# Two-layer PEER encoder kernel: scores of four heads at the 11th query block, and the search in two parts

## The reference, cut to what matters

```
q = (ht @ w_q).reshape(T, PEER_HEADS, 2, PEER_HALF_DIM)      # 8 heads, two halves of 128
scores = einsum('thic,hikc->thik', q, sub_keys)              # 128 keys for each half
sv, si = top_k(scores, 16)
cand = sv[:, :, 0, :, None] + sv[:, :, 1, None, :]
best, ci = top_k(cand.reshape(T, 8, 256), 16)
expert = i1 * 128 + i2;  gate = softmax(best)                # 128 experts for each token
hid = gelu(x . w_down[expert]);  out = sum(gate * hid * w_up[expert])
```

## Time and profile before

| | us |
|---|---|
| median of 3 runs | 1507.93 (1506.27 to 1508.06) |
| the profiled execution, whole | 1518.31 |
| its span | 1516.5 |
| PE busy | 1485.6 |
| DVE busy | 886.0 |
| POOL busy | 715.4 |
| ACT busy | 476.5 |
| granted TensorE clock, mean | 0.997 |

### The profile page before, as it was taken

The page is one execution under the profiler, slowest core; times in us unless marked ns, Lnnn a source line. Parts: engine busy times, 40 slices in busy tenths (PEclk is TensorE's granted clock), DMA queues, the critical chain, the costliest instruction groups (busy, mean ns, idle before and its releaser), DMA issues.

```text
span 1516.5 us, 29050 instructions
## 1 busy us (share of the span) xinstructions
PE 1485.6 (98%) x10668; PEld 1445.1 (95%) x10668; DVE 886.0 (58%) x2901; ACT 476.5 (31%) x1200; POOL 715.4 (47%) x632
## 2 busy tenths in 40 slices
PE   7999999999999999999999999999999999999996
PEld 6889999999999999999988999999999999999995
DVE  1740989947885444444623339997488834444463
ACT  5654231238881000000156532221688500000001
POOL 6577033348995233333457731333699823323350
PEclk9999999999999999999999999999999999999999
DMA  6456988999999999999945579899999999999993
GB/s 239 147 193 230 333 316 334 408 408 352 388 380 404 416 416 416 417 417 414 361 139 202 205 247 344 320 409 409 363 374 383 387 418 415 416 417 417 416 399 131
DMA packets 126417, 523.12 MB, mean 345 GB/s; under 512 B 14817, under 2 KB 15073, under 8 KB 109537
## 3 DMA queue, kind: packets, MB, share of 16 engines
q1 hardware_dynamic: 56896, 240.27, 41.8%
q0 software_dynamic: 55296, 201.35, 34.0%
q10 hardware_dynamic: 14112, 80.04, 12.9%
HBM read 519.48 MB, written 1.05 MB: 343 GB/s over the span
## 4 chain that ended last, share of the span: by engine, by line
PE 91%; DMA 3%; issue 2%; ACT 2%; POOL 2%; DVE 0%; DVEq 0%; ACTq 0%; POOLq 0%
PE ps L993 90%; DMA spare<-in_wu 1%; POOL w_lo L599 1%; DMA arena<-in_rows,ret 1%; PE ps L1001 1%; ACT w_hi L686 0%; DMA xs<-in_x 0%; ACT arena L674 0%; DMA raw<-in_wm 0%; POOL arena L616 0%; ACT arena L745 0%; ACT hT_hi L701 0%; ACT L664 0%; DVE arena L1510 0%; ACT ret L903 0%
## 5 line engine op out<-in xcount | busy, mean ns | idle before, releaser
L993 PE MATMUL ps<-arena,w_raw 128*128 128x160 f32 (+1 forms) x2688 | 381.1, 300 | 4.0 <-issue 2.3
L993 PE MATMUL ps<-arena,raw 128*128 128x160 f32 (+1 forms) x2688 | 377.5, 299 | 0.2
L993 PEld LDWEIGHTS ps<-arena,w_raw 128*128 128x128 f32 x2688 | 369.7, 191 | 6.3 <-issue 6.2
L993 PEld LDWEIGHTS ps<-arena,raw 128*128 128x128 f32 x2688 | 368.1, 190 | 0.7 <-issue 0.7
L616 POOL DMA_INDIRECT arena<-in_up_rows,ret x192 | 187.4, 976 | 358.5 <-DVE oh_buf L1684 267.0
L616 POOL DMA_INDIRECT arena<-in_rows,ret x192 | 199.9, 1041 | 295.1 <-ACT ret L880 104.5
L1684 DVE SCALAR_TENSOR_TENSOR oh_buf<-arena,ret,oh_buf 128x1024 f32<-128x1024 f32 x126 | 161.9, 1285 | 230.2 <-DMA arena<-in_up_rows,ret 224.6
L599 POOL TENSOR_TENSOR w_lo<-raw,w_hi 128x1024 fp32r<-128x1024 f32 x80 | 194.0, 2434 | 93.3 <-PE ps L993 66.3
L993 PE MATMUL ps<-arena 128*128 128x160 f32 (+5 forms) x1336 | 184.5, 302 | 2.1 <-DMA spare<-in_wu 2.1
L993 PEld LDWEIGHTS ps<-arena 128*128 128x128 f32 (+2 forms) x1336 | 177.9, 189 | 5.8 <-issue 4.4
L1567 DVE SCALAR_TENSOR_TENSOR arena<-arena,ps 128x1024 f32<-128x1024 f32 x128 | 153.6, 1212 | 0.0
(11 more groups left out here) (146 smaller groups left out, 1788.4 us busy)
## 6 DMA issues: line engine op xcount, KB each, us to landing
raw<-in_wd SPq DMA_DIRECT2D x92, 512.0 KB
w_raw<-in_wd SPq DMA_DIRECT2D x92, 512.0 KB
raw<-in_wm SPq DMA_DIRECT2D x80, 512.0 KB
low_rows<-in_wu SPq DMA_DIRECT2D x18, 1024.0 KB
arena<-in_wu SPq DMA_DIRECT2D x18, 1024.0 KB
arena<-in_wd SPq DMA_DIRECT2D x32, 512.0 KB, 5.0
raw<-in_wu SPq DMA_DIRECT2D x14, 1024.0 KB
raw<-in_wu ACTq DMA_DIRECT2D x14, 1024.0 KB
```

The costliest lines, as they stand in the source:

```text
L993: return nc.tensor.matmul(out, lhsT, rhs, start=start, stop=stop, skip_group_check=shared)
```

## The change

**Scores of four heads early.** Before the 11th query block (`b == EARLY_SCORES_BEFORE` = 10) PE computes tile 0's scores of heads 0 to 3, into banks 0 and 1; ACT copies them after `high` of block 12. The other scores follow after the query blocks; tile 0's heads 4 to 7 use banks 0 and 1 again and wait for ACT's copies.

**Search in parts.** DVE searches heads 0 to 3 of tile 0, then heads 4 to 7, then tile 1. The first part uses PSUM banks 2 and 3, so the row products of tile 0 (`h_rows`, banks 2 and 3, before down block 8) now wait for `pair_found` of that part. Dots are put from the last steps of the second part on: 44 in 20 places. A piece of picks is now two neighbouring heads (heads i and i + 4 before).

**Places.** The pieces are taken before blocks 4, 7, 20 and 25 (18, 21, 24 and 26 before), ids at 71 (77), gates from block 74 (80), the dots of the gate stage are 52 over 50 blocks (56 over 44). The ring starts at slot 2, since slots 0 and 1 lie on the scores of tile 0, and POOL's tenth gather waits until both parts of the scores have been searched. SP may load the up pair that lies on ring slots 8 and 9 after 88 dots (90 before).

```diff
-RING, IN_FLIGHT = 10, 5
+RING, IN_FLIGHT, RING_FIRST = 10, 5, 2
...
-IDS_AT = 77
-TAKE_AT = 26
-PIECES, PIECE_AT = 4, (18, 21, 24, 26)
-MORE_AT, MORE_TAKE_AT, MORE_GATES_AT = 28, 33, 40
+IDS_AT = 71
+TAKE_AT = 28
+PIECES, PIECE_AT = 4, (4, 7, 20, 25)
+EARLY_SCORES_BEFORE, EARLY_HEADS = 10, RH // 2
+SCORE_BANKS = (0, 1, 0, 1, 4, 5, 6, 7)
+MORE_AT, MORE_TAKE_AT, MORE_GATES_AT = 26, 34, 40
-G_FROM = 80
+G_FROM = 74
-ONES_FROM, ROWS_AT, ONES = 12, 8, 432
-SPARSE_FIRST, MORE_LAST = 18, 10
-EARLY, EARLY_PLACES = SPARSE_FIRST + MORE - MORE_LAST, 14
+ONES_FROM, ROWS_AT, ONES = 30, 8, 432
+SPARSE_FIRST, MORE_LAST = 26, 14
+EARLY, EARLY_PLACES = SPARSE_FIRST + MORE - MORE_LAST, 20
-    return EARLY + max(0, min(ROWS - EARLY, (b - G_FROM - 1) * (ROWS - EARLY) // 44))
+    return EARLY + max(0, min(ROWS - EARLY, (b - G_FROM - 1) * (ROWS - EARLY) // 50))
...
-        slot = q % RING if q < ROWS else (q - ROWS) % UP_RING
+        slot = (q + RING_FIRST) % RING if q < ROWS else (q - ROWS) % UP_RING
...
-        first_sv = ps[:, 5, 0:P].rearrange("p (h k) -> p h k", h=RH)
-        first_id = ps[:, 5, P:2 * P].rearrange("p (h k) -> p h k", h=RH)
+        def search_psum(bank, heads):
+            firsts = ps[:, bank, 0:2 * heads * TOPK].rearrange("p (i h k) -> p i h k", i=2, h=heads)
+            pay = ps[:, bank + 1, 0:heads * CAND].rearrange("p (h c) -> p h c", h=heads)
+            return firsts[:, 0], firsts[:, 1], pay
...
-                sp.wait_ge(row_used, l * GATHERS + ROWS - ROWS % RING)
+                sp.wait_ge(row_used, l * GATHERS + ROWS - (ROWS + RING_FIRST) % RING)
...
+                    if q == RING - 1:
+                        pool.wait_ge(first_searched, l + 1)
...
+                def take_scores(i):
+                    act.wait_ge(sc_psum, 8 * l + i + 1)
+                    nc.scalar.activation(scores[i // 4][:, i % 4 * 512:(i % 4 + 1) * 512], ps[:, SCORE_BANKS[i], :],
+                                         ACT.Copy, scale=rinv[:, 2, i // 4:i // 4 + 1]).then_inc(sc_sb, 1)
+
                 take_queries(0)
-                high_parts(l * LAYER + Q_FROM + 12, l * LAYER + MIX_BLOCKS)
+                act.wait_ge(rinv_done, query_norm)
+                for b in range(Q_FROM + 12, MIX_BLOCKS):
+                    high(b)
+                    if b == Q_FROM + EARLY_SCORES_BEFORE + 2:
+                        take_scores(0)
+                        take_scores(1)
                 take_queries(1)
-                act.wait_ge(rinv_done, query_norm)
-                for i in range(8):
-                    act.wait_ge(sc_psum, 8 * l + i + 1)
-                    nc.scalar.activation(scores[i // 4][:, i % 4 * 512:(i % 4 + 1) * 512], ps[:, i, :], ACT.Copy,
-                                         scale=rinv[:, 2, i // 4:i // 4 + 1]).then_inc(sc_sb, 1)
+                for i in range(2, 8):
+                    take_scores(i)
 
                 def take_hidden(b):
...
-                        first = half * PICKS + i * size
+                        first = (2 * i + half) * size
...
                     transpose_half(xs, 4, hT_psum, k, HALF_BANKS)
+                def score(t, halves):
+                    for n in halves:
+                        o = n % 4 * P
+                        last = mm(ps[:, SCORE_BANKS[4 * t + n // 4], o:o + P], qT[:, n, t * P:(t + 1) * P],
+                                  subk[:, n, :])
+                        if n % 4 == 3:
+                            last.then_inc(sc_psum, 1)
...
+                    if b == EARLY_SCORES_BEFORE:
+                        pe.wait_ge(subk_loaded, 16 * (l + 1))
+                        pe.wait_ge(qT_sb, 8 * l + 4)
+                        score(0, range(2 * EARLY_HEADS))
                     if b == NORMED_BEFORE:
                         pe.wait_ge(hn_done, QUARTERS * (l + 1))
...
-                pe.wait_ge(subk_loaded, 16 * (l + 1))
-                for t in range(TILES):
-                    for n in range(HALVES):
-                        if n % 4 == 0:
-
-                            pe.wait_ge(qT_sb, 8 * l + (8 if t else max(4, n // 2 + 2)))
-                        o = n % 4 * P
-                        last = mm(ps[:, 4 * t + n // 4, o:o + P], qT[:, n, t * P:(t + 1) * P], subk[:, n, :])
-                        if n % 4 == 3:
-                            last.then_inc(sc_psum, 1)
+                for n in range(2 * EARLY_HEADS, HALVES, 4):
+                    pe.wait_ge(qT_sb, 8 * l + n // 2 + 2)
+                    pe.wait_ge(sc_sb, 8 * l + n // 4 - 1)
+                    score(0, range(n, n + 4))
+                pe.wait_ge(qT_sb, 8 * (l + 1))
+                score(1, range(HALVES))
...
                     if b < SLOTS:
-                        pe.wait_ge(sc_sb, 8 * l + DOWN_BANKS[slot] + 1)
+                        pe.wait_ge(sc_sb, 8 * l + 3 + slot)
...
-                pe.wait_ge(sc_sb, 8 * l + 4)
+                pe.wait_ge(pair_found, PIECES * l + PIECES // 2)
...
-
-                for t in range(TILES):
-                    dve.wait_ge(sc_sb, 8 * l + 4 * (t + 1))
+                def early_dot():
+                    if not early[0]:
+                        dve.wait_ge(h_rows_psum, l + 1)
+                        dve.wait_ge(more_rows_sb, 16 * PARTS * (l + 1))
+                    dots(early_after(early[0] - 1), early_after(early[0]))
+                    early[0] += 1
+
+                def search(t, h0, h1, ready, bank, dots_from):
+
+                    heads, halves = slice(h0, h1), range(2 * h0, 2 * h1)
+                    first_sv, first_id, pay = search_psum(bank, h1 - h0)
+                    dve.wait_ge(sc_sb, 8 * l + ready)
                     top16([(scores[t][:, n * KEYS:(n + 1) * KEYS], sv[:, t, n, :], si[:, t, n, :])
-                           for n in range(HALVES)], t)
+                           for n in halves], t, dots_from < 1)
                     settle()
-                    step(nc.vector.tensor_copy(sif[:, t].rearrange("p h i k -> p (h i) k"), si[:, t]))
-                    svt = sv[:, t].rearrange("p (h i) k -> p h i k", i=2)
-                    if t == 0:
+                    found_ids = nc.vector.tensor_copy(
+                        sif[:, t, heads].rearrange("p h i k -> p (h i) k"), si[:, t, 2 * h0:2 * h1])
+                    if t == 0 and h0:
+                        found_ids.then_inc(first_searched, 1)
+                        dve.wait_ge(first_searched, l + 1)
                         dve.wait_ge(sc_sb, 8 * (l + 1))
                         dve.wait_ge(hng_done, l + 1)
                         step(nc.vector.tensor_copy(numbers, iota[:, :]))
...
-                        h = j // 4 + j // 2 % 2 * (RH // 2)
+                        h = j // 2
...
-                            early_dot(t)
+                        if j % 2 and dots_from < 3:
+                            early_dot()
...
+                gates_of(1)
 
                 dve.wait_ge(idg_psum, l + 1)
                 step(nc.vector.tensor_copy(gT, ps[:, 5, 0:SEQ]))

```

More of the change, by code:

```diff
@@ L886, in take_gates @@
                     for half in range(2):
-                        here, picks = slice(half * SPARSE, (half + 1) * SPARSE), slice(half * PICKS, (half + 1) * PICKS)
-                        nc.scalar.activation(row_gate[here], bb[0:SPARSE, picks], ACT.Copy).then_inc(gates_taken, 1)
+                        here = slice(half * SPARSE, (half + 1) * SPARSE)
+                        picks = bb[0:SPARSE, 0:P].rearrange("p (i h k) -> p h i k", h=2, k=TOPK)[:, half]
+                        nc.scalar.activation(row_gate[here].rearrange("p (i k) -> p i k", k=TOPK), picks,
+                                             ACT.Copy).then_inc(gates_taken, 1)
                 def take_more_picks():
@@ L1523, in _, with top16 @@
                 norm_tokens()
-                def top16(rows, t):
+                def top16(rows, t, with_dots):
                     for r in range(0, len(rows), 8):
@@ L1598, in _ @@
                         na = a1 - a0
-                        for dst, first, second in ((cand, first_sv, svt), (pay, first_id, sif[:, t])):
+                        for dst, first, second in ((cand[:, heads], first_sv, svt), (pay, first_id, ids)):
                             d = dst[:, :, o:o + na * nb].rearrange("p h (a b) -> p h a b", b=nb)
-                            f = first[:, :, a0:a1].unsqueeze(3).to_broadcast([P, RH, na, nb])
-                            s = second[:, :, 1, 0:nb].unsqueeze(2).to_broadcast([P, RH, na, nb])
+                            f = first[:, :, a0:a1].unsqueeze(3).to_broadcast([P, h1 - h0, na, nb])
+                            s = second[:, :, 1, 0:nb].unsqueeze(2).to_broadcast([P, h1 - h0, na, nb])
@@ L1603, in _ @@
                             step(nc.vector.tensor_tensor(d, f, s, ALU.add))
                         o += na * nb
[L1605 removed]
+                    top16([(cand[:, h, :], best[:, t, h, :], ci[:, t, h, :]) for h in range(h0, h1)], t, dots_from < 2)
                     settle()
[L1607 to L1608 removed]
```

(15 more changed lines are left out.)

37 lines of the change are left out of this document (18 added, 19 removed).

## The result

The changed kernel takes 1513.5 us (median; 1510.49 to 1517.14), the kernel before 1506.05 (1505.04 to 1508.06) beside it: ratio 1.0051, 95% interval 1.0042 to 1.006. It is slower by 0.5% where 1503.1 us was forecast, and it lies above the range. The profiled execution of the changed kernel took 1516.39 us with a span of 1514.6, which is 3 us over its median. That of the kernel before had been 12 us over its own, and this turns out to matter.

A forecast was written before the change was run, and what follows sets the result against it. PE was taken as the bound, busy for 1485.6 of 1516.5 us, so only its short waits could be won: 0.3 - 1.7 - 1.6 - 0.3 - 1.5 = -4.8, from the median 1507.9 to 1503.1 us. The range was 1496 to 1512.

The forecast's parts named there:

- The steps up to the gathers: Tile 0's early scores and search: first maximum at 135.5 us instead of 154.61, gathers from near 166 instead of 199.
- the waits for picks: Down blocks 0 to 30: pieces of picks are found before ACT takes them, 4 us of lateness covered; cost 0.
- The POOL rival: POOL's low parts beside the search stretch from 2.40 to 3.9 us: 8 us slower, 1511; chance 0.04.
- the lock that the prediction cites: Skill's rule: DVE operations with two SBUF inputs, or in a two-port mode, lock GpSimd out for their whole length; search priced 0.
- -1.7, -1.6, -0.3 and -1.5: PE waits expected to go: layer 1's first one-hots, end of down blocks, gate-stage issue gaps, up blocks' spare pair; in us.
- The rival "nothing is gained": PE's few waits may be the profiler's, or full DMA takes the time back: 1507.5 us; chance 0.22.
- The step on the gathers: Unused DMA time at 185 to 245 us, 5.8 MB, takes 11 gathers; layer 1's one-hot wait goes: -1.7 us.
- The gathers' gain: Last gather before the first one-hots issued 21.7 us earlier, needed 13.0 earlier; new margin 8.7, saving 1.7 us.
- The burst: Ten gathers at once from POOL, now at 166 us: stalls of 4.4 and 1.6 us stay, taken as 0.
- one rival: The burst's stalls go, as DVE's and PE's programs are elsewhere at 166 us: -6.0, 1497.1 us; chance 0.17.
- The slower rival: Burst and buffer fill starve PE at half speed, 10 us in each layer: +14, 1517 us; chance 0.09.

The follow-up runs named there:

- the kernel with later pairs: Changed kernel, with the first two pairs of up blocks (2.1 MB) queued ahead of down block 80 instead of 24: 1505.32 us, ratio 0.9944 to the kernel before.
- the trace at 1507.73 us: The kernel before, run unchanged for a trace on the chip of the third group of experiments: 1507.73 us.
- all three traces with early gathers and early pairs on one load queue: Changed kernel at first (1513.5 us) and on another chip (1513.88), and changed kernel with first gates back at block 80 (1512.22), all with up pairs ahead of block 24.
- the traces at 1515.15 and 1507.73 us: The kernel before, run unchanged for traces on two chips: 1515.15 us on one, 1507.73 us on the other.

## Why the prediction was wrong

The steps up to the gathers were right. DVE's first maximum came at 135.23 us (135.5 forecast), ACT fitted the two copies in, the first gather left at 164.70 (166), the waits for picks were covered, and DVE was done with tile 1 at 308.1, at 304.9 in the kernel with later pairs (300.3), still ahead of block 71. The POOL rival fell, since its parts beside the search take what they took alone:

```profile
135.23 1.65 DVE L1555 MAX8 oh_buf<-arena 128x8 f32<-128x128 f32 x8 [21.59 <-ACT arena L855]
```

```profile
140.37 2.41 POOL L603 TENSOR_TENSOR w_lo<-raw,w_hi 128x1024 fp32r<-128x1024 f32 x1 [0.47 <-PE ps L1008]
164.70 1.11 POOL L622 DMA_INDIRECT arena<-in_rows,ret  x1 [16.16 <-ACT ret L893]
```

L1497 had stretched these parts by 1.76 us for 4.63 us of its own work. That agrees in direction with the lock that the prediction cites, but doesn't show one for the whole length of L1497.

**The gains were not in the median.** The sum took -1.7, -1.6, -0.3 and -1.5 from waits of one profiled execution that stood 10.4 us above the median, and carried them over "if those waits are there as well". They were not: the trace at 1507.73 us has 0.6 us of them, and the kernel with later pairs, with none, is 1.3 us faster where the kernel before takes 1506.2, for 4.8 in the sum. The rival "nothing is gained" had this right. Its reason, the profiler, isn't borne out: the trace at 1507.73 us is of a profiled execution too, and on three other chips the kernel before has a median of 1513 to 1516 us.

**The unused DMA time was spent twice.** The step on the gathers filled 185 to 199 and 216 to 245 us, where DMA stood at 284 and 265 GB/s, with 11 gathers, and took it as free. The mean rate said so. But the loads shared one queue, and a second busy queue takes half of the packets whatever the first one needs; 204 GB/s were left against a need of 241. I costed the loads at nothing, and named no cover for them. The cover was the lead of 16 blocks, and it ran out at block 39. It cost 7.7 us in layer 0, 3 of them the clock. This is the step that failed most: with one load of 2.1 MB moved out of that queue the kernel takes 1505.3 instead of 1513.5 us, and the waits of PE for down weights, there in all three traces with early gathers and early pairs on one load queue, are gone.

**The gathers' gain was mis-sized.** 21.7 us earlier was forecast for the last gather ahead of layer 1's one-hots, 13.0 needed, and 12.75 measured (1077.33 to 1064.58), while PE came 14.4 us earlier (1078.26 to 1063.86). The lead of 11 gathers was there, 32 against 21 by 250 and by 992 us. But from the 32nd to the 53rd one took 3.3 us in layer 0 and 3.6 in layer 1, instead of 3.1. The loads moved no more than before in that time (17.5 and 17.4 MB from 992 to 1064 us); the gathers moved 11.1 MB for 11.9, at 398 GB/s in all for 409, and why isn't shown. So the -1.7 became a wait of 3.40 for 1.73, where I had said that a third of the lead could be lost.

**The burst.** I took 0, "these stay", and argued that the gather burst does harm where DMA is full. The reverse holds: its gaps come when the gathers have the transfers almost alone. In the changed kernel the burst stands beside loads at a half share, and the stalls went, as one rival said, though not for its reason, the place in the program. The slower rival's price was near (+14; in the profiled execution the two waits cost 7.7 + 3.4 = 11.1 us beside the kernel with later pairs, whose span is 11.5 us shorter; by the medians it is 8.2), but by luck: it had PE starved at the burst in both layers, and the damage came 80 us after it and in two forms. I gave it 0.09 because DMA at 407 GB/s had held PE full for 86 us, and overlooked that two load queues stand there against the gathers, with 30.5 and 29.0% of the transfers to 42.5%.

What stays open: how a gather queue that runs alone starves PE in the middle of a block. That it is PE's instruction stream fits gaps without a releaser, and no run here shows it. Nor do they show what makes the load queue idle or busy beside the burst from chip to chip, which goes with the difference between 1506 and 1515 us.

## What to carry to other kernels

Before a stream of gathers is moved into free transfer time, count the queues that will be busy and give each an equal share of the packets; compare the load queue's share, not the mean rate, with what the engine reads, and see for how many blocks the lead covers the difference. Here one postponed load of 2.1 MB turned +0.5% into -0.1% where the kernel before takes 1506 us, and -0.2% into -0.6% where it takes 1515, while a second load queue moved the wait to the gathers. When the profiled execution is well above the median, the waits in it may be absent from the runs that the median is made of: look at a second trace before you put them in a sum, and treat a gain made of them as one on some chips only.

## What was not expected of the hardware

The same kernel takes 1506 us on some chips and 1513 to 1516 on others, at a granted clock of 0.997 or 0.998 in the three traces read. More than half of the difference is PE's gaps beside the bursts of gathers: between the traces at 1515.15 and 1507.73 us the spans differ by 7.5 us, and the windows of the two bursts by 34 matmuls, 4.6 us; the rest is in longer waits at the gates and at the end of the down blocks. Two busy queues had equal shares of the packets, to a few counts in 1736. And two gathers in flight are far too few here: one went out each 4.1 us from 271.80 to 296.22, 7.4 us from issue to landing, and with PE waiting for them the traffic from 300 to 360 us fell to 292 GB/s, where five in flight had 387.
